# Token sums kept in memory by accumulating scatters, with the closing rows and the delta-rule transposes reordered

## The reference, cut to what matters

```python
h = x + hybrid_mixer(rms_norm(x), ...)                  # q, k, v, z, decay; chunked delta rule; gates; projections
xn = rms_norm(h)
top_vals, top_idx = lax.top_k(xn @ w_router + b_router, 4)
top_w = softmax(top_vals)
# for each token's 4 experts e:
gu = xn @ w_gate_up[e] + b_gate_up[e]
hid = (clip(gu[:, D:], -7, 7) + 1) * g * sigmoid(1.702 * g)     # g = min(gu[:, :D], 7)
y_e = hid @ w_down[e] + b_down[e]
h = h + sum over the 4 experts of top_w[e] * y_e
out = rms_norm(h, norm_final_g)
```

## Time and profile before

| | us |
|---|---|
| median of 3 runs | 1846.33 (1846.29 to 1846.99) |
| the profiled execution, its own time | 1846.1 |
| its span, first to last instruction | 1844.4 |
| PE busy | 1803.5 (98% of the span) |
| DVE busy | 1469.7 (80%) |
| ACT busy | 1101.8 (60%) |
| POOL busy | 409.3 (22%) |

### The profile page before, as it was taken

The page is one execution under the profiler, slowest core; times in us unless marked ns, Lnnn a source line. Parts: engine busy times, 40 slices in busy tenths (PEclk is TensorE's granted clock), DMA queues, the critical chain, the costliest instruction groups (busy, mean ns, idle before and its releaser), DMA issues.

```text
span 1844.4 us, 23922 instructions
## 1 busy us (share of the span) xinstructions
PE 1803.5 (98%) x8636; PEld 1500.2 (81%) x8636; DVE 1469.7 (80%) x1095; ACT 1101.8 (60%) x902; POOL 409.3 (22%) x338
## 2 busy tenths in 40 slices
PE   8999999999999999999999999999999999999995
PEld 6888888897888887888888888888888888888873
DVE  4336667674334689999999999999999999999996
ACT  4223562333322447777777777777777777777771
POOL 1000111410000027223223222321322322232231
PEclk9999999999999999999999999999999999999998
DMA  5223423004762548999999999999999999999976
GB/s 185 92 92 130 144 92 115 21 27 160 252 216 88 231 157 325 375 383 359 374 380 373 353 382 378 350 378 379 358 366 384 368 358 380 378 346 380 382 281 242
DMA packets 129806, 507.80 MB, mean 275 GB/s; under 512 B 26359, under 2 KB 26567, under 8 KB 95652
## 3 DMA queue, kind: packets, MB, share of 16 engines
q1 hardware_dynamic: 118144, 490.62, 69.7%
q0 software_dynamic: 9280, 16.27, 2.3%
q10 hardware_dynamic: 2340, 0.33, 0.1%
HBM read 492.46 MB, written 32.02 MB: 284 GB/s over the span
## 4 chain that ended last, share of the span: by engine, by line
PE 91%; DVE 4%; ACT 2%; issue 1%; DMA 1%; POOL 0%; SPq 0%; DVEq 0%; POOLq 0%; ACTq 0%
PE PB L2337 12%; PE PB L2338 12%; PE PB L2340 12%; PE PB L2256 11%; PE PB L2361 6%; PE PB L2358 6%; PE PB L2359 6%; PE PB L1941 4%; PE PB L1943 4%; PE PB L1942 4%; PE PB L2074 2%; PE PB L2327 2%; PE PB L2315 1%; PE PB L2321 1%; PE PB L2221 1%; DVE acc L1423 1%
## 5 line engine op out<-in xcount | busy, mean ns | idle before, releaser
L520 DVE TENSOR_TENSOR mlo<-mraw,mhi 128x2048 fp32r<-128x2048 f32 x384 | 906.6, 2395 | 48.2 <-ACT mhi L516 46.6
L516 ACT ACTIVATE mhi<-mraw 128x2048 fp32r<-128x2048 f32 x384 | 721.5, 1914 | 109.9 <-PE PB L2340 109.9
L2337 PE MATMUL PB<-mhi,xgT_hi 128*128 128x512 f32 x1024 | 402.7, 393 | 1.4 <-DVE mlo L520 1.4
L2338 PE MATMUL PB<-mlo,xgT_hi 128*128 128x512 f32 x1024 | 399.7, 390 | 0.0
L2340 PE MATMUL PB<-mhi,xgT_lo 128*128 128x512 f32 x1024 | 273.9, 389 | 0.0
L2337 PEld LDWEIGHTS PB<-mhi,xgT_hi 128*128 128x128 f32 x1024 | 192.7, 188 | 42.2 <-DVE mlo L520 1.4
L2340 PEld LDWEIGHTS PB<-mhi,xgT_lo 128*128 128x128 f32 x1024 | 192.2, 188 | 40.3
L2338 PEld LDWEIGHTS PB<-mlo,xgT_hi 128*128 128x128 f32 x1024 | 192.7, 188 | 39.5
L2358 PE MATMUL PB<-mhi,hT_hi 128*128 128x512 f32 x512 | 202.1, 395 | 1.1 <-DVE hT_lo L1836 1.1
L2359 PE MATMUL PB<-mlo,hT_hi 128*128 128x512 f32 x512 | 199.4, 389 | 0.0
L893 POOL TENSOR_TENSOR glu<-glu 128x1024 f32<-128x1024 f32 x32 | 78.9, 2464 | 521.7 <-DVE glu L1831 521.7
(11 more groups left out here) (360 smaller groups left out, 2564.6 us busy)
## 6 DMA issues: line engine op xcount, KB each, us to landing
mraw<-in_w_gate_up_dram SPq DMA_DIRECT2D x256, 1024.0 KB, 8.0
mraw<-in_w_down_dram SPq DMA_DIRECT2D x128, 1024.0 KB, 7.9
raw<-in_w_in_dram SPq DMA_DIRECT2D x27, 1024.0 KB, 5.1
qkvT<-in_w_in_dram SPq DMA_DIRECT2D x8, 1024.0 KB, 5.1
expert_rows_scratch<-zeros SPq DMA_DIRECT2D x4, 2048.0 KB, 11.5
mraw<-expert_rows_scratch SPq DMA_DIRECT2D x6, 1024.0 KB, 11.5
qkvT<-in_w_o_gdn_dram SPq DMA_DIRECT2D x4, 1024.0 KB, 6.5
qkvT<-in_w_o_sconv_dram SPq DMA_DIRECT2D x4, 1024.0 KB, 5.1
```

Of the source, the lines that this page charges most:

```text
L516: nc.scalar.activation(mhi[split_slot(m)][:], mraw[:, raw_slot(m), :], ACT.Copy).then_inc(e_h, 1)
L520: nc.vector.tensor_tensor(mlo[split_slot(m)][:], mraw[:, raw_slot(m), :], mhi[split_slot(m)][:].bitcast(F32), ALU.subtract).then_inc(e_l, 1)
L2337: pe.matmul(gate_up_bank[:, n, :], xgT_hi[:, k, :], w_hi[:, n, :], start=False, stop=False)
L2338: pe.matmul(gate_up_bank[:, n, :], xgT_hi[:, k, :], w_lo[:, n, :], start=False, stop=False)
```

## The change

The scratch `y_d` goes. In its place `sum_d` holds one row for each token (and 128 rows past them for the empty slots). SP stores `h_rows` into it ahead of the loop; only the 128 extra rows are zeroed. ACT scales an item's rows by their weights as it copies them out of PSUM, with the weights fetched for each item by a further small indirect DMA (`slot_weights`). The scatter adds its rows in memory. In the loop POOL does `gather(i+3)` ahead of `scatter(i)`, and the scatter takes all 128 slots. Behind the loop SP loads 4 tiles of 512 KB of sums into `h_rows`; the last item's rows come in as a high and a low part in float32r, with a 0/1 `put_back` that DVE makes; all four additions come ahead of the four `finish` steps; the last tile is finished and stored in halves. In the delta rule `turn_blocks(c + 2)` stands ahead of the sums of squares. The numbers in `row` are 4 apart so that the empty slots' targets shifted by two bits fall in the 128 extra rows.

```diff
# SP
-                        if 2 <= g <= TT + 1:
+                        if g == 2:
                             sp.wait_ge(s_zeros, 1)
-                            sp.dma_start(y_d... [g - 2] ..., zeros ...to_broadcast([P, TOPK * D // GW, GW])).then_inc(s_ycl, 16)
+                            sp.dma_start(sum_d[SEQ:]..., zeros ...to_broadcast([P, D // GW, GW])).then_inc(s_ycl, 16)
...
+                    for t in range(TT):
+                        sp.dma_start(sums_by_token[:, t, :], h_rows[:, t, :]).then_inc(s_hout, 16)
...
                     for t in range(TT):
-                        (waits on e_l, e_used for the raw slots)
-                        for half in range(2):
-                            sp.dma_start(rows_t[t]...[:, w], y_by_token[t][:, w]).then_inc(s_pick[t][half], 16)
+                        sp.dma_start(h_rows[:, t, :], sums_by_token[:, t, :]).then_inc(s_back[t], 16)
                     for t in range(TT):
-                        sp.wait_ge(s_out, t + 1)
-                        sp.dma_start(out_d[:, t, :], h_rows[:, t, :]).then_inc(s_st, 16)
+                        for n, w in enumerate(parts_of(t)):
+                            sp.wait_ge(s_out, t + n + 1)
+                            sp.dma_start(out_d[:, t, w], h_rows[:, t, w]).then_inc(s_st, 16)
# POOL
                     def scatter(i):
-                        nc.gpsimd.tensor_copy(now[:, 1:2], target[:, bass.ds(i, 1)]).then_inc(s_goal, 1)
+                        nc.gpsimd.tensor_copy(now[:, 1:2], index[:, bass.ds(i, 1)]).then_inc(s_goal, 1)
+                        pool.wait_ge(s_ws, 16 * i + 16)
+                        nc.gpsimd.tensor_copy(now[:, 2:3], target[:, bass.ds(i + 1, 1)]).then_inc(s_wrow, 1)
                         pool.wait_ge(s_goal, i + 1)
+                        pool.wait_ge(s_wrow, i + 2)
                         pool.wait_ge(s_y, i + 2)
                         step()
-                        nc.gpsimd.indirect_dma_start(y_d, ...(ap=now[:, 1:2], axis=0), y_rows[:], None,
-                                                     bounds_check=SEQ * TOPK - 1, oob_is_err=False).then_inc(s_yst, 16)
+                        nc.gpsimd.indirect_dma_start(sum_d, ...(ap=now[:, 1:2], axis=0), y_rows[:], None,
+                                                     compute_op=ALU.add, bounds_check=SEQ + P - 1, oob_is_err=True
+                                                     ).then_inc(s_yst, 16)
+                        slot_weights()
                         pool.wait_ge(s_yst, 16 * i + 16)
                         pool.sem_inc(s_yfree, 1)
+                    def slot_weights():
+                        nc.gpsimd.indirect_dma_start(slot_weight, None, w_d, ...(ap=now[:, 2:3], axis=0),
+                                                     bounds_check=SEQ * TOPK - 1, oob_is_err=False).then_inc(s_ws, 16)
...
-                    (four by_weight diagonals, put_back by POOL)
+                    pool.wait_ge(s_hout, 16 * TT)
                     with pool.Fori(0, last) as i:
                         pool.wait_ge(s_th, i + 1)
                         hidden(i + 1)
-                        scatter(i)
                         pool.wait_ge(s_tx, i + 2)
                         gather(i + 3)
+                        scatter(i)
# ACT
                         act.wait_ge(s_yfree, i + 1)
-                        nc.scalar.activation(y_rows..., y_bank, ACT.Copy).then_inc(s_y, 1)
+                        act.wait_ge(s_ws, 16 * i + 16)
+                        nc.scalar.activation(y_rows..., y_bank, ACT.Copy, scale=slot_weight).then_inc(s_y, 1)
...
+                    act.wait_ge(s_ws, 16 * last + 16)
                     for n in range(2):
-                        nc.scalar.activation(y_rows[...], y_bank[:, n, :], ACT.Copy).then_inc(s_ylast, 1)
+                        nc.scalar.activation(last_hi[...], y_bank[:, n, :], ACT.Copy, scale=slot_weight).then_inc(s_ylast, 1)
# DVE, delta rule
+                    if c + 2 < TT:
+                        turn_blocks(c + 2)
                     for g in BOTH:
                         dve.wait_ge(s_osq, 2 * c + g + 1)
...
-                    if c + 2 < TT:
-                        turn_blocks(c + 2)
# DVE, behind the loop
-                    (add_rows: 12 scalar_tensor_tensor over the tokens' rows)
                     def add_products(t):
+                        dve.wait_ge(s_back[t], 16)
                         dve.wait_ge(s_bo, 2 * t + 2)
                         nc.vector.tensor_tensor(h, PM[...], h, ALU.add).then_inc(s_sum, 1)
+                    nc.vector.tensor_scalar(put_back[:], iota_tok[:], goal_f[:, 0:1], None, ALU.is_equal)
+                    for n in range(2):
+                        dve.wait_ge(s_ylast, n + 1)
+                        nc.vector.scalar_tensor_tensor(out=last_lo[:, half_row], in0=y_bank[:, n, :], scalar=slot_weight,
+                                                       in1=last_hi[:, half_row]..., op0=ALU.mult, op1=ALU.subtract)
                     for t in range(TT):
                         add_products(t)
+                    dve.wait_ge(s_sum, TT)
+                    for t in range(TT):
                         finish(t)
# PE, behind the loop
                         for n in range(2):
                             pe.wait_ge(s_ylast, n + 1)
                             pe.matmul(PM[...], put_back[...], last_hi[...], start=False, stop=False)
+                            pe.wait_ge(s_last_lo, n + 1)
+                            pe.matmul(PM[...], put_back[...], last_lo[...], start=False, stop=True).then_inc(s_bo, 1)
-                    (fourth_rows: by_weight times the tokens' fourth rows, for 4 tiles)
```

More of the change, by code:

```diff
@@ L558, in hybrid_block, with parts_of @@
         count_bank = PM[:, bank3(0, LAST), TT * E:(TT + 1) * E]
[L560 to L563, removed]
         BANK_OF_TILE = (0, 2, 6, 4)
-        y_by_token = y_d.rearrange("(t p k) d -> t p (k d)", p=P, k=TOPK)
+        sums_by_token = sum_d[0:SEQ].rearrange("(t p) d -> p t d", p=P)
+        slot_weight = goal_f[:, 1:2]
         fsq = glu[:, 1, :]
+        def parts_of(t):
+            return [slice(0, D)] if t < LAST else [slice(0, GW), slice(GW, D)]
         def last_item(eng):
@@ L1286, in y_copy @@
                         act.wait_ge(s_yfree, i + 1)
-                        nc.scalar.activation(y_rows[:].rearrange("p (b c) -> p b c", b=2), y_bank, ACT.Copy).then_inc(s_y, 1)
+                        act.wait_ge(s_ws, 16 * i + 16)
+                        nc.scalar.activation(y_rows[:].rearrange("p (b c) -> p b c", b=2), y_bank, ACT.Copy,
+                                             scale=slot_weight).then_inc(s_y, 1)
                     first_tokens_hi()
@@ L1324, in mix_and_experts @@
                     act.wait_ge(s_yfree, last + 1)
+                    act.wait_ge(s_ws, 16 * last + 16)
                     for n in range(2):
-                        nc.scalar.activation(y_rows[:, n * GW:(n + 1) * GW], y_bank[:, n, :], ACT.Copy).then_inc(s_ylast, 1)
+                        nc.scalar.activation(last_hi[:, n * GW:(n + 1) * GW], y_bank[:, n, :], ACT.Copy,
+                                             scale=slot_weight).then_inc(s_ylast, 1)
                     for t in range(TT):
@@ L1863, in mix_and_experts @@
                     weights_lo(dve, last, 3)
-                    added = [0]
-                    def add_rows(t, ks):
-                        for k in ks:
-                            dve.wait_ge(s_pick[t][k * 2 // TOPK], 16)
-                            wait(dve, s_added, added[0])
-                            n = t * TOPK + k
-                            nc.vector.scalar_tensor_tensor(out=h_rows[:, t, :], in0=rows_t[t][:, k, :], scalar=weight[:, n:n + 1],
-                                                           in1=h_rows[:, t, :], op0=ALU.mult, op1=ALU.add).then_inc(s_added, 1)
-                            added[0] += 1
                     def add_products(t):
+                        dve.wait_ge(s_back[t], 16)
                         dve.wait_ge(s_bo, 2 * t + 2)
-                        dve.wait_ge(s_added, added[0])
                         h = h_rows[:, t, :].rearrange("p (b c) -> p b c", b=2)
@@ L2426, in mix_and_experts @@
                     last_rows(3)
-                    for t in range(1, TT):
-                        fourth_rows(t)
                 mix_and_experts()
```

85 lines of the change are left out of this document (34 added, 51 removed).

## The result

| | before | after |
|---|---|---|
| median, us | 1846.31 (1846.08 to 1846.99, 4 runs) | 1826.26 (1825.68 to 1826.51, 4 runs) |
| ratio after / before | | 0.9889, 95% interval 0.9878 to 0.9901 |
| span of the profiled execution, us | 1844.4 | 1824.2 |
| DMA engines busy, 1064 to 1418 us | 0.95 | 1.00 |

What follows compares the result with a forecast made beforehand. PE was taken to bound nearly everything except two delta-rule waits and the tail. From a span of 1844.4, less 2.7 (delta rule) and 17.8 (tail), came 1823.9, plus 1.7 and 0.2 a median of 1825.8, said as 1826; range 1820 to 1839.

Steps and rivals of the forecast that it cites:

- Delta rule: Delta rule's chunk ends: turning blocks earlier removes PE's 1.43 us wait twice; bounds 1.4 (DVE) and 2.9 (PE), taken 2.7.
- Ahead of the loop: Before the loop: dropped fills and new `h_rows` stores are worth nothing; uncovered, the stores would cost 5 us once.
- Loop, POOL: POOL in the loop: the later scatter and weights' gather delay nobody, with 14 us of slack on POOL, 18 on ACT.
- Loop, DMA: DMA in the loop: 0.7 to 1.9 us added an item fits a free share of 3.2 us; effect 0.
- the decision point: Loop's DMA: added DMA time of about 3 us an item, from which the loop would lose time.
- The two reads of the adding: Scatter's adding: two source reads halve the rate; the loop's term stays 0, speaking against the change only through the tail's landing.
- Tail: Behind the loop: scatter issued at 1800.5, landed 5.0 us later, DVE done at 1822.4, span end 1826.6; gives 17.8 us.
- the loads bind, by a us: Tail: loaded sums reach DVE at 1812.3, PE's first products at 1811.4, so the loads decide when additions start.
- The halves: Tail's last tile: with a half tile to store, the span ends 4.2 us behind DVE's last step instead of 4.4.
- Rival 1: Scatter lands late, rows serial at 14.4 us, hidden in the loop, or up to 2.5 us behind DVE's splits; 1835.5; chance 0.18.
- Rival 2: Loop: adding holds the DMA engines, DMA-bound from about 3 us over plain; 112 us lost, 1938; chance 0.10.
- Rival 4: Tail's gain bound elsewhere: PE or the final stores take 4 us more, 1830; its chance is inside the forecast's 0.64.

Runs made afterwards that it cites:

- e2: The kernel before with only the `turn_blocks` call moved ahead of the sums of squares: 1844.0 us, ratio 0.9985.
- e1: The kernel after with `turn_blocks(c + 2)` put back behind the sums of squares: 1828.28 us.
- e5: The kernel after with the item's scatter put back ahead of the gather in POOL's loop: 1859.73 us, ratio 1.0074 to before.
- e8: The kernel before with SP storing 1 MB more in each item: 1877.93 us.
- e7: The kernel after with SP storing 1 MB more in each item: 1894.70 us.
- e3: The kernel after with the scatter overwriting rows instead of adding (`compute_op` left out, `oob_is_err` False): 1829.32 us.
- e4: The kernel after with the scatter's row limit set so that empty slots move nothing: 1826.49 us.
- e11: The kernel after with POOL's last iteration written out without its gather: 1825.94 us.
- e9: The kernel after with the last tile finished and stored whole instead of in halves: 1825.44 us.
- e12: The kernel after without POOL's last gather, with the final norm's factor on ACT and DVE and the gain loaded before the landing wait: 1824.64 us, ratio 0.9882 to before.

## Why the prediction was right, and where not

- **Delta rule, 2.7 us.** Measured 2.7 between the same matmuls, in after and in e2. It was a choice between bounds of 1.4 and 2.9, and PE carries the stage, as the upper one had it. PE's wait on `T` is gone; about 0.2 us a chunk is paid back where PE's products with `o` now run beside DVE making it (1.26 us in place of 1.04).
- **Ahead of the loop, nothing.** Right: from the third stage's first product to the last item's `hidden` the four kernels before, after, e1 and e2 take 1365.96 to 1366.00 us.
- **Loop, POOL.** Right in its effect: the landing went from 7.4 to 11.9 us and nobody waited (the 1365.96 us again), and e5 shows that this rests on the gather standing first. The prediction leaned on the gather's slack without a price for losing it.
- **Loop, DMA: the right zero from a wrong size.** "Free share: (1.03 - 0.94) x 35.4 = 3.2 us" is the step that failed. 1.03 was read in 6 us of one item; over a whole stretch the loops that are short of DMA reach 0.98 and 1.01 (e8, e7). By the extra stores the free time was 1.7 us, and the decision point lay there and not at 3. The added time was 1.2 us by the stores, inside the 0.7 to 1.9 of the prediction, and 1.8 and 2.0 by the share and the queue, at its upper end. So 0.5 us was left, and with 1.9 us by the stores' measure some 0.2 us an item or 6 us would have been lost. That the zero held was in part luck.
- **The two reads of the adding.** The Trainium skill (Collectives: The Full Stack, "The bandwidth ceiling") says that the two source reads halve the rate of a reduce. The engines' time agrees with that. Take a plain scatter of 128 rows as P, one of half the rows as P/2, and the gathers as G, in per cent of the engines' span for POOL's queue: e3 has P + G = 3.4 and before P/2 + G = 2.3, so P is 2.2 and G 1.2, and the adding scatter is 5.8 - 1.2 = 4.6, twice P; with half the rows it would be 3.5 in all, and e4 shows 3.6. This is an estimate from rounded shares. The landing behind the issue, 8.05 - 3.55 = 4.5 us with adding and 5.3 - 2.96 = 2.3 without, has the same ratio but is no rate: e4's is unchanged at half the rows, and so is the plain one's (3.3 - 1.08 = 2.2 before). In the prediction the rule changed no term; the reading counted in full stood in the upper 1.9 us.
- **Tail, 17.8 us.** Measured 17.8, but the terms missed and cancelled. The landing was taken at 5.0 us and was 8.05, over the 8 us that the prediction itself had named as a sign of being wrong: 1.9 of the 3.1 us is POOL's issue, which took 3.55 us beside DVE's splits where e11's took 1.65, and the rest the adding (2.75 over plain in e3, where 1.6 was taken). The issue was put at 1800.5 in the clock of before, 1798.1 in that of after, and came at 1796.06, because the two copies and the step took 0.18 to 0.19 us each and not "1.2" and "1.6". SP's 1.0 us behind the landing was 0.3. From there the chain holds up to DVE's additions: "the loads bind, by a us" is the 0.9 us from 1809.4 to 1810.27. Behind them two more terms cancel. DVE's last step ended at 1820.9 and not at 1820.0, having waited 0.46 us for a factor that POOL took 1.46 us to make and not 0.56. And the span ended 3.3 us behind DVE and not 4.2: the 4.4 of before was POOL's drain and not the store, for SP was done 2.9 us behind DVE there.
- **The halves.** "With a half tile to store 4.2" in place of 4.4: e9 shows 0.1.
- **Rival 1** had the issue beside DVE nearly right (1.9 us against its "up to 2.5") and the serial rows wrong: e4 moved fewer rows at the same landing. The 7.4 against 3.4 us that it read as a sign of the port is none: both issues took 1.07 to 1.08 us, and the DMA engines were busy for 0.94 of the time in the loop and 0.06 from 1790 to 1800. **Rival 2** was nearer than its 0.10 said: its point was at 1.7 us of engine time by the extra stores. **Rival 4** named PE or the stores as the next bound; e3, e11 and e12 show PE 0.9 us behind. What ended the span in fact was on no list: POOL's drain, by 1.3 us before (it ended at 1844.1, SP was done at 1842.8) and 0.5 after.

## What to carry to other kernels

Read how full a resource is from long stretches, and its ceiling from a kernel that is short of it, not from the highest short sample. Even so a share can be too coarse; a dummy transfer in both kernels measures what is left. Measure a small gain between two instructions that both kernels have around the edit: there the move was 2.7 us in both pairs, where the medians said 2.0 and 2.6. When a scatter becomes dependent on newer data, ask what stands behind it in its queue: here the order of two calls was worth 33.5 us, more than the change itself. In a tail, look for the second chain and for what each engine does last before shortening the first: 3.4 us off the scatter's landing gave 0.3, no more than the runs' spread.

## What the runs showed of the hardware

- **POOL's closing drain.** It started with POOL's last operation and took 4.6 to 8.6 us (4.61 in e12, 5.97 in after, 8.62 in e3), while DVE's took 1.3 to 1.5 and ACT's 0.3 to 1.2. An engine whose last small operation comes late in the span can end it. Part of the length is the last operation itself (1.46 us in after, 0.56 in e3 and before, 0.19 in e12). Less that it is 4.4 to 4.5 us in after and in all its variants but e3, 5.5 in before, e2 and e8, and 8.1 in e3; what sets these three values is open.
- **POOL beside DVE.** A copy of 128 x 1 took 2.25 us beside DVE's split of two SBUF tiles and 0.19 beside `hT_lo`, which reads PSUM. The adding scatter's issue took 1.65 us in e11, begun 1.3 us ahead of a split, and 3.55 in after, begun within one. So an issue 1.6 us earlier landed 3.4 us earlier: 1.9 us of it is the shorter issue. The Trainium skill (SBUF — State Buffer, "SBUF: two separate sides") says that a DVE instruction with two SBUF inputs holds the port pair it shares with GpSimd for its whole length against a GpSimd instruction that reads SBUF. The copies agree, down to the PSUM input, which leaves DVE with only one from SBUF. The scatter's issue, which reads its row numbers from SBUF, fits the same rule: 3.50 us in the loop and 3.55 in the tail when begun within a split, 1.65 when begun ahead of one. What the section says of descriptors that GpSimd can't write, it says of DVE's 2-port modes, and no row here shows such a mode.
- **An adding scatter.** About 2.2 us more from the issue's end to the landing than a plain one, 0.6 us more of POOL's issue, and 5.8% of the engines' time in place of 3.4% for POOL's queue as a whole. By the estimate above the scatter itself takes twice the engines' time of a plain one. With fewer rows really moved (e4) the first two stayed and only the share fell, to 3.6%.
